# Softmax of an encoder step: minima of negated scores, maxima and low halves by turns, and a head's scaling moved to GpSimd

## What is computed

```
def sink_softmax(s, sink):
    m = jnp.maximum(jnp.max(s, axis=-1, keepdims=True), sink)
    e = jnp.exp(s - m)
    return e / (jnp.sum(e, axis=-1, keepdims=True) + jnp.exp(sink - m))
...
    s = jnp.einsum('bqkgd,bqskd->bkgqs', qg, kg).astype(jnp.float32) * SCALE
    s = jnp.where(valid[:, :, None, None, :], s, NEG)
    p = jax.nn.softmax(s, axis=-1)
```

## Time and profile before

| | |
|---|---|
| Median of three runs | 1899.58 us (1897.05 to 1901.8) |
| Profiled execution, its own time | 1900.48 us |
| Its span | 1898.7 us |
| PE busy | 1832.2 us (96% of the span) |
| DVE busy | 1112.3 us (59%) |
| ACT busy | 607.3 us (32%) |
| POOL busy | 372.4 us (20%) |

### The profile page before, as it was taken

How to read it: one execution, slowest core, us unless ns; L and a number is a source line. 1 busy time by engine, 2 the same in 40 slices (tenths; PEclk the granted TensorE clock), 3 DMA queues, 4 the chain that set the end, 5 groups by cost and what they waited for, 6 DMA issues and landing times.

```text
span 1898.7 us, 30572 instructions
## 1 busy us (share of the span) xinstructions
PE 1832.2 (96%) x11609; PEld 1780.1 (94%) x11609; DVE 1112.3 (59%) x1868; ACT 607.3 (32%) x1006; POOL 372.4 (20%) x299
## 2 busy tenths in 40 slices
PE   5999999999999998989899999999999999999997
PEld 4899999989999997777899999999999999999997
DVE  6257878978788686889663444553244452245443
ACT  4232122268511226777724211111011111011132
POOL 2112212256533324222320001110001110011100
PEclk8999999999999999999999999999999999999998
DMA  4111111110111114211213111111111111111112
GB/s 145 34 34 46 39 34 50 49 35 23 34 50 50 37 45 107 51 34 46 62 51 137 44 36 53 44 44 50 50 34 44 44 44 56 44 34 46 45 42 93
DMA packets 167458, 96.73 MB, mean 51 GB/s; under 512 B 7676, under 2 KB 163596, under 8 KB 167372
## 3 DMA queue, kind: packets, MB, share of 16 engines
q1 hardware_dynamic: 166396, 93.57, 17.0%
q0 software_dynamic: 976, 2.00, 0.4%
HBM read 89.55 MB, written 5.99 MB: 50 GB/s over the span
## 4 chain that ended last, share of the span: by engine, by line
PE 89%; DVE 5%; ACT 2%; issue 2%; DMA 1%; POOL 1%; SPq 0%; DVEq 0%; ACTq 0%
PE ps L954 75%; PE ps L1063 3%; PE ps L966 3%; PE ps L1086 3%; PE ps L1201 2%; PE ps L1161 2%; DVE probs L2078 1%; DVE key_mask L1893 1%; DVE top L1893 1%; DMA x_rows<-in_x_prompt 0%; PE ps L1027 0%; DVE h_rows L1814 0%; ACT probs L1549 0%; PE ps L1028 0%; DMA w_raw_in_lo<-in_w_in 0%
## 5 line engine op out<-in xcount | busy, mean ns | idle before, releaser
L954 PE MATMUL ps<-h_hi,w_hi 128*128 128x352 f32 (+1 forms) x1944 | 424.4, 326 | 3.9 <-POOL w_lo L770 3.9
L954 PE MATMUL ps<-h_hi,w_lo 128*128 128x352 f32 (+1 forms) x1944 | 420.3, 324 | 0.0
L954 PE MATMUL ps<-h_lo,w_hi 128*128 128x352 f32 (+1 forms) x1944 | 420.0, 324 | 0.0
L954 PEld LDWEIGHTS ps<-h_hi,w_hi 128*128 128x128 f32 (+1 forms) x1944 | 330.4, 189 | 6.8 <-issue 5.1
L954 PEld LDWEIGHTS ps<-h_hi,w_lo 128*128 128x128 f32 (+1 forms) x1944 | 334.1, 188 | 0.5
L954 PEld LDWEIGHTS ps<-h_lo,w_hi 128*128 128x128 f32 (+1 forms) x1944 | 330.8, 188 | 0.5
L1334 ACT ACTIVATE w_hi<-w_raw 128x1024 fp32r<-128x1024 f32 (+1 forms) x128 | 124.2, 971 | 245.7 <-PE ps L954 245.5
L923 POOL TENSOR_TENSOR t<-t,t 128x1056 f32<-128x1056 f32 x22 | 54.3, 2469 | 631.4 <-ACT t L1695 631.4
L1893 DVE MAX8 top<-key_mask 128x8 f32<-128x768 f32 (+5 forms) x192 | 170.6, 890 | 11.8 <-PE ps L954 1.2
L770 POOL TENSOR_TENSOR w_lo<-w_raw,w_hi 128x1024 fp32r<-128x1024 f32 (+1 forms) x53 | 100.5, 1896 | 354.5 <-ACT w_hi L1334 354.5
L1893 DVE MATCH_REPLACE8 key_mask<-top,key_mask 128x768 f32<-128x768 f32 (+5 forms) x192 | 167.8, 877 | 0.9 <-issue 0.9
(11 more groups left out here) (266 smaller groups left out, 2968.0 us busy)
## 6 DMA issues: line engine op xcount, KB each, us to landing
w_raw_in_lo<-in_w_in SPq DMA_DIRECT2D x56, 256.0 KB, 2.8
w_raw<-in_w_in SPq DMA_DIRECT2D x54, 256.0 KB, 3.0
w_raw<-in_w_gate SPq DMA_DIRECT2D x44, 256.0 KB, 3.0
w_raw<-in_w_up SPq DMA_DIRECT2D x44, 256.0 KB, 3.0
w_raw<-in_w_down SPq DMA_DIRECT2D x32, 256.0 KB, 2.9
w_raw_in_lo<-in_w_in SPq DMA_DIRECT2D x44, 128.0 KB, 2.2
x_rows<-in_x_prompt SPq DMA_DIRECT2D x8, 512.0 KB, 8.3
w_raw<-in_w_out SPq DMA_DIRECT2D x16, 256.0 KB, 3.1
```

The costliest lines, as they stand in the source:

```text
L954: last = nc.tensor.matmul(PS[0:rows, NB * k + b, 0:e - a], w[:, k, t, 0:rows], x[:, t, a:e], start=m == 0 and w is WHI and x is hi, stop=m ...
```

## The change

1. `mask_max` scales by −SCALE and keeps the minimum of the negated scores, which is the negated maximum, straight in the place that `exp` reads as its bias; `exp` scales by −1. In the window attention the reduction starts from the negated sink, in the sparse one from 3.4e38. The masks are added as before. The negations L2083, the combining operation L2106, the copies of the sample's sinks and the semaphore `negated` go; `exp` waits for its own head's maximum.
2. In sparse steps the two maxima stand by turns with the low halves: maximum 0, low half 0 (and in odd steps the running sum), maximum 1, low half 1. For pairs that are one ahead both reciprocals move in front of low half 2.
3. For the sixteen pairs that are one ahead, head 0 is scaled by POOL, behind the split of chunk 2 where there is one.

```
@@ pairs
-                            mask = None if window else MASK_S[:, :]
-                            sinks, negative = SINK_S[:, :], NEG_SINK[:, NH:NH + NKV]
+                            mask = MASK0[:, 0:n] if window else MASK_S[:, :]
+                            negative = NEG_SINK[:, NH:NH + NKV]
@@ POOL
-                    nc.gpsimd.tensor_copy(columns, pair["sinks"].unsqueeze(2)).then_inc(sink_in, 1)
+                    nc.gpsimd.tensor_copy(columns, pair["negative"].unsqueeze(2)).then_inc(sink_in, 1)
...
             def normalise(pair):
-                pool.wait_ge(inverse, 2 * pair["x"] + 2)
+                pool.wait_ge(inverse, 2 * pair["x"] + (2 if pair["window"] else 1))
                 p = probs_of(pair, 0)
                 inv = stat[:, pair["ub"], 5, 0:1].broadcast_to([P, pair["n"]])
                 nc.gpsimd.tensor_tensor(p, p, inv, ALU.mult).then_inc(probs[0], 1)
...
             for y, pair in enumerate(SPARSE):
-                for c in range(len(pair["chunks"])):
-                    sparse_split(y, c)
+                after = SPARSE[y + 1] if y + 1 < len(SPARSE) else None
+                for c in range(max(len(pair["chunks"]), 3)):
+                    if c < len(pair["chunks"]):
+                        sparse_split(y, c)
+                    if c == 2 and after and after["ahead"] == 1:
+                        normalise(after)
@@ ACT, exp
-                act.wait_ge(negated, 2 * x + (2 if pair["window"] else h + 1))
+                act.wait_ge(masked, 2 * x + h + 1)
...
-                nc.scalar.activation(p, p, ACT.Exp, bias=stat[:, ub, 1, h:h + 1],
+                nc.scalar.activation(p, p, ACT.Exp, scale=-1.0, bias=stat[:, ub, 1, h:h + 1],
@@ DVE, mask_max
-                top, neg = stat[:, ub, 0, h:h + 1], stat[:, ub, 1, h:h + 1]
-                out = probs_of(pair, h)
-                if pair["mask"] is None:
-                    V_.tensor_scalar(out, scores_of(pair, h), SCALE, None, ALU.mult, ALU.max,
-                                     accum_out=top).then_inc(masked, 1)
-                else:
-                    V_.tensor_tensor_reduce(out=out, in0=scores_of(pair, h), in1=pair["mask"], scale=SCALE,
-                                            scalar=-3.4e38, op0=ALU.add, op1=ALU.max,
-                                            accum_out=top).then_inc(masked, 1)
-                if not window:
-                    dve.wait_ge(masked, 2 * x + h + 1)
-                    V_.tensor_scalar(neg, top, -1.0, None, ALU.mult).then_inc(negated, 1)
+                V_.tensor_tensor_reduce(out=probs_of(pair, h), in0=scores_of(pair, h), in1=pair["mask"], scale=-SCALE,
+                                        scalar=pair["negative"][:, h:h + 1] if window else 3.4e38,
+                                        op0=ALU.add, op1=ALU.min,
+                                        accum_out=stat[:, ub, 1, h:h + 1]).then_inc(masked, 1)
@@ DVE, invert
-                if h == 0:
+                if h == 0 and pair["ahead"] == 2:
@@ DVE, window_step
-                    dve.wait_ge(masked, 2 * x + 2)
-                    V_.scalar_tensor_tensor(stat[:, ub, 1, :], stat[:, ub, 0, :], -1.0, ahead["negative"],
-                                            ALU.mult, ALU.min).then_inc(negated, 2)
@@ DVE, attend
-                        if ahead:
-                            mask_max(ahead, 0)
-                            mask_max(ahead, 1)
                         for c in range(max(count, 4)):
+                            if c < 2 and ahead:
+                                mask_max(ahead, c)
+                            if c == 2 and after and not early:
+                                invert(after, 0)
+                                invert(after, 1)
                             if c < count:
                                 pt_low(pair, c)
                             if c == 0 and y > 0 and ps[y - 1]["last"]:
                                 output(ps[y - 1])
-                            if c <= 1 and after and not early:
-                                invert(after, c)
```

More of the change, by code:

```diff
@@ L346, in build @@
         SINK = keep("sinks", NH)
-        SINK_S = keep("sinks_sample", NKV)
         TOP8 = keep("top8", 24)
@@ L386, in build @@
         q_hi = sem("q_hi")
-        s_done, masked, negated, exp_done = sem("s_done"), sem("masked"), sem("negated"), sem("exp_done")
+        s_done, masked, exp_done = sem("s_done"), sem("masked"), sem("exp_done")
         sink_in, inverse = sem("sink_in"), sem("inverse")
@@ L495, in pairs @@
                             head = g * NJ + 2 * half
-                            sinks, negative = SINK[:, head:head + 2], NEG_SINK[:, head:head + 2]
+                            negative = NEG_SINK[:, head:head + 2]
                         size = 1 if sample else 2
@@ L500, in pairs @@
                         out.append(dict(x=x, i=i, g=g, half=half, sample=sample, window=window, n=n,
-                                        first=first_block, chunks=chunks, q=q, mask=mask, sinks=sinks, negative=negative, ub=x % 3,
+                                        first=first_block, chunks=chunks, q=q, mask=mask, negative=negative, ub=x % 3,
                                         o=o, last=sample or half == 1))
@@ L1825, in _ @@
             for j in range(NJ):
-                V_.tensor_copy(SINK_S[DEC * j:DEC * (j + 1), :], SINK[DEC * j:DEC * (j + 1), j:NH:NJ])
                 V_.tensor_scalar(NEG_SINK[DEC * j:DEC * (j + 1), NH:NH + NKV],
@@ L2101, in window_step @@
                 if ahead:
-                    x, ub = ahead["x"], ahead["ub"]
                     mask_max(ahead, 0)
                     mask_max(ahead, 1)
-                    dve.wait_ge(masked, 2 * x + 2)
-                    V_.scalar_tensor_tensor(stat[:, ub, 1, :], stat[:, ub, 0, :], -1.0, ahead["negative"],
-                                            ALU.mult, ALU.min).then_inc(negated, 2)
                 if pair:
```

## The result

| | before | changed |
|---|---|---|
| Median | 1899.37 us (15 runs, 1897.05 to 1904.21) | 1904.84 us (15 runs, 1902.46 to 1910.97) |
| Ratio | | 1.0031, 95% interval 1.0022 to 1.0041 |
| Profiled execution, its own time | 1900.48 us | 1904.03 us |
| Span | 1898.7 us | 1902.2 us |

The account below looks back on a forecast made before the run. PE bounds the window stage; some 22 us of PE idle in the sparse stage is all the change can win. Terms 0 + 5.3 − 0.5 − 5.5 + 1.2 = +0.5 us gave 1900.1 us, range 1891 to 1908.

Parts of the forecast that it names:

- Tiles 0 and 1: Eight one-chunk steps: the second maximum behind the running sum delays PE's scores at four places; net +5.3 us.
- the 2.0 that I took: Tiles 0 and 1: part of the 7.3 us delay given back, as 2.9 us of old waits are already over.
- Tiles 3 and 4: Two-chunk steps: the later maximum is not late and low halves come one maximum earlier; −0.5 us.
- Tiles 5 to 7: Eleven steps: DVE loses negations and head 0's scaling, and the running sum comes earlier; net −5.5 us.
- the four steps with a split: Steps 17, 18, 19 and 23: GpSimd's scaling behind its split of chunk 2 ends late for PE's transposes; together +0.8 us.
- Step 17: In tiles 5 to 7: split plus scaling end at 824.6, against transposes starting at 822.72; +1.9 us.
- the −6.3 of the seven other steps: Tiles 5 to 7, steps without a split: each gains the lesser of PE's idle time and DVE's lost work.
- Tile 2: Two chunks, 384 keys: GpSimd's 0.83 us scaling replaces DVE's 0.42 on the chain in three of four pairs; +1.2 us.
- A: Rival: all of DVE's relief counts, all 11.96 us of idle time in tiles 5 to 7 goes; 1891.5 us, chance 0.21.
- B: Rival: sum before second maximum costs the full +7.3 in tiles 0 and 1, GpSimd scales slowly; 1907.7 us, chance 0.16.
- C: Rival: DVE and GpSimd stop each other, GpSimd's scaling holding DVE up for its whole length; 1913.6 us, chance 0.05.
- D: Rival: nothing measurable because no part reaches PE; 1899.6 us, chance 0.58 together with the forecast.

Follow-up runs that it names:

- kernels 2: The changed kernel with, for pairs two ahead, the order maximum 0, low half 0, maximum 1, running sum; 1900.0 us.
- Experiment 3: The changed kernel with head 0 scaled by DVE again for all sparse pairs; 1903.8 us.
- 10: The changed kernel profiled once more, nothing altered; 1904.3 us (one run).
- kernels 5: The changed kernel with GpSimd's scaling ahead of its split of chunk 2 instead of behind it; 1903.3 us.
- 9: The kernel before with turns in the steps that prepare pairs two ahead (tiles 0 to 4) and nothing else; 1909.1 us.
- Experiment 4: The kernel before with minima of negated scores alone: no negations, no turns, head 0 scaled by DVE, reciprocals where they were; 1896.0 us.
- kernel 1: The changed kernel with both maxima ahead of the low half again for pairs two ahead (tiles 0 to 4); 1895.7 us.
- kernel 7: As kernel 6, but GpSimd scales head 0 of pairs 17 to 28, ahead of its split of chunk 2; 1891.1 us.
- kernel 6: Minima everywhere, turns and later reciprocals only in steps preparing pairs 17 to 28, both maxima first elsewhere, head 0 scaled by DVE; 1893.0 us.

## Why the prediction was right in its range and short in its sum

**Tiles 0 and 1: the wait was right, the clock was left out.** Forecast +5.3, measured +7.7. The four places where PE's scores wait for the second maximum are in the trace of the changed kernel where they were forecast:

```profile
736.70 0.33 PE L1164 MATMUL ps<-k_hi,q_hi 64*128 64x128 f32 x2 [1.01 <-DVE softmax_stats L2074]
...
745.20 0.39 PE L1164 MATMUL ps<-k_hi,q_hi 64*128 64x256 f32 x2 [2.46 <-DVE softmax_stats L2074]
...
754.68 0.39 PE L1164 MATMUL ps<-k_hi,q_hi 64*128 64x256 f32 x2 [2.57 <-DVE softmax_stats L2074]
...
765.38 0.50 PE L1164 MATMUL ps<-k_hi,q_hi 64*128 64x512 f32 x2 [2.01 <-DVE softmax_stats L2074]
```

They are 1.0, 2.5, 2.6 and 2.0 us, in sum 8.1. At the third PE had waited before, too, for 0.9 us:

```profile
748.91 0.39 PE L1161 MATMUL ps<-k_hi,q_hi 64*128 64x256 f32 x2 [0.93 <-DVE softmax_stats L2078]
```

So 1.0, 2.5, 1.6 and 2.0 are new, in sum 7.1; forecast were 1.1, 2.3, 1.7 and 2.2, in sum 7.3. At the place of the earlier trace rows the chain reads as it was written: ACT's copy, DVE's sum, the maximum, and 0.06 us behind its end PE's scores at 745.20.

```profile
743.50 0.59 ACT L1337 ACTIVATE attn_sum<-ps 64x512 f32<-64x512 f32 x1
...
744.12 0.68 DVE L2124 TENSOR_TENSOR attn_sum<-ps,attn_sum 64x512 f32<-64x512 f32 x1 [3.43 <-ACT attn_sum L1337]
...
744.73 0.41 DVE L2074 CUSTOM_DVE_ANT_0 probs<-ps,mask_causal 128x256 f32<-128x256 f32 x1
```

Of this 1.2 is given back, not the 2.0 that I took: the two other old waits for maxima (2.0 us together) are still there with 1.8, and what went is a wait of 1.0 put down to issue. 7.1 − 1.2 makes, with rounding, the 6.0 us of new idle time. So the net term was 0.7 short by what is given back, and the missing 1.7 is the lower clock, which stands nowhere in my sum. Here are two pieces of tiles 0 and 1 of the changed kernel, and two of tile 2:

```profile
740.00:745.00 5.00, 2.75 (x25) 2.54 (x23) 1.45 (x5) 3.02 (x8) 2.55 (x2) 1.00 0.52 133
745.00:750.00 5.00, 4.80 (x30) 4.67 (x31) 3.18 (x13) 3.92 (x11) 2.52 (x2) 0.68 0.12 28
940.00:944.00 4.00, 2.70 (x18) 2.25 (x17) 2.31 (x7) 3.02 (x8) 2.12 (x2) 1.00 0.11 32
944.00:948.00 4.00, 3.64 (x16) 3.67 (x17) 0.69 (x1) 2.28 (x6) 1.28 (x1) 0.60 0.00 0
```

In 740 to 745 PE was busy for 2.75 of 5 us, at 1.00. In the next five it was busy for 4.80, with a granted clock of 0.68, so for most of them at the lower of its two levels, 1.2 GHz instead of 2.4. The same again in tile 2: 2.70 of 4 us busy, then 0.60. In both places the holes come first and the work behind them is slow. That makes a hole dearer than its length. How much dearer differs: against the 32.7 us of the kernels whose clock stays at 1.00, PE is busy for 1.7 to 1.9 us longer in kernels 2, 3, 10 and the changed one, and for 4.5 in kernels 5 and 9, which idle 10.2 and 10.5 us in tiles 0 and 1 where the changed one idles 10.2. That the holes bring the lower clock fits every profile here; no run changed one and held the other.

**Tiles 3 and 4.** Forecast −0.5, measured −1.1. Experiment 4 shows 0.9 of it with minima alone; I had counted the negations in tiles 5 to 7 only. The turns themselves gave 0.3 there (43.7 in experiments 1 and 4, 43.5 changed).

**Tiles 5 to 7: the size was right, its parts were not.** Forecast −5.5, measured −5.3. By parts: minima −3.4 (experiment 4), turns and late reciprocals −3.0 (experiment 3 against 4), GpSimd's scaling as placed +1.1 (the change against experiment 3). These parts are what each gave when added in this order; GpSimd's scaling without turns was not run. I had taken the scaling's relief of DVE for the main gain. What I had of it at the four steps with a split was right: the scaling's durations are those worked out from the slope, 1.46, 1.67, 1.89 and 0.83,

```profile
L829 POOL TENSOR_TENSOR probs<-probs,softmax_stats 128x1024 f32<-128x1024 f32 x4 | 7.6, 1894 | 1.8 <-DVE softmax_stats L2084 1.8
L829 POOL TENSOR_TENSOR probs<-probs,softmax_stats 128x896 f32<-128x896 f32 x4 | 6.7, 1684 | 1.0 <-DVE softmax_stats L2084 1.0
L829 POOL TENSOR_TENSOR probs<-probs,softmax_stats 128x768 f32<-128x768 f32 x4 | 5.9, 1464 | 1.0 <-DVE softmax_stats L2084 1.0
...
L829 POOL TENSOR_TENSOR probs<-probs,softmax_stats 128x384 f32<-128x384 f32 x4 | 3.3, 828 | 1.4 <-DVE softmax_stats L2084 1.4
```

and the splits push it past the start of the transposes. Step 17, at which I expected +1.9 (without taking off its idle 0.5, as I did at the other three): the split, the scaling, two search operations of DVE beside it, and then PE's transposes.

```profile
828.08 1.30 POOL L778 TENSOR_TENSOR w_lo<-w_raw_in_lo,w_hi 128x512 fp32r<-128x512 f32 x1 [3.89 <-ACT w_hi L1337]
...
829.33 1.47 POOL L829 TENSOR_TENSOR probs<-probs,softmax_stats 128x768 f32<-128x768 f32 x1
829.53 0.56 DVE L1895 MAX8 top<-key_mask 128x8 f32<-128x384 f32 x1
...
830.27 0.54 DVE L1895 MATCH_REPLACE8 key_mask<-top,key_mask 128x384 f32<-128x384 f32 x1
...
830.86 0.66 PE L969 MATMUL ps<-ident,probs 128*128 128x128 f32 x4 [1.61 <-POOL probs L829]
```

PE's transposes had to wait 1.6 us there, 1.6 and 1.3 in the next two steps, and 0.4 in step 23, against 1.9, 1.7, 0.85 and 0.1 of overshoot in the forecast. What failed inside the term is the −6.3 of the seven other steps: it took DVE's whole loss, up to 1.3 us a step, as PE's gain. That −5.5 came so near to −5.3 is luck: the negations and the turns gave 6.4, and the scaling, which I had taken for the main gain, cost 1.1. Experiment 3 has the scaling on DVE and eleven steps of 97.5 us, and with GpSimd's scaling well placed they take 95.6 (kernels 5 and 7): 8 us of DVE's work, taken away, gave PE 1.9.

**Tile 2: the cause was wrong.** Forecast +1.2 for GpSimd's slower scaling, measured +2.6: 1.0 more idle time and 1.6 more busy time, of which 1.4 is the clock (29.57 us busy in kernel 1, at 1.00, against 30.93). Experiment 3 keeps the waits with DVE's scaling and has 34.3, where experiment 4 has 32.6. Of these 1.7, 0.6 is there in kernel 6 without turns in tile 2, so it must come from the changed stretch ahead, and 1.1 belongs to the turns with the later reciprocals. GpSimd's scaling, with 34.0 in kernel 1 against 34.3, is 0.3 the better one: my term had the wrong sign.

**The sum.** +0.5 was forecast, +3.8 is what the four stretches show, and 3.1 of the 3.3 between them is clock (1.7 in tiles 0 and 1, 1.4 in tile 2). The other errors (+0.7 in tiles 0 and 1, −0.6 in 3 and 4, +0.2 in 5 to 7) nearly cancel. The medians are 5.5 apart, since the profiled execution of before was 1.1 above its median and that of the changed kernel 0.8 below.

**The rivals.** A (all of DVE's relief is PE's gain) is out: PE still idles 7.5 us in tiles 5 to 7, and even in kernel 7, where no split is in the way, 4.2. B was right in its place: the sum in front of the second maximum. Its terms for GpSimd at a slow pace were not: 1024 took 1.89 us, not 2.44 (and its sum leaves out the −0.5 of tiles 3 and 4). C is out: in the fence above a search maximum and a replacement of DVE, 0.56 and 0.54, ran beside GpSimd's scaling at their usual length (552 and 543 ns on average), and a low half of 512 that ran beside one (853.48, within the scaling of 853.07 to 854.75) took 0.69 us, the average being 0.69 too. The Trainium skill (SBUF — State Buffer, "SBUF: two separate sides") names DVE operations in a 2-port mode or with two inputs from SBUF as those that meet GpSimd, and these rows agree that a search or a low half, which reads one operand from PSUM, isn't among them. What did stretch is DVE's own scaling, from SBUF to SBUF: at 256 elements it took, in the changed kernel, 1.11 us at 748.87, during a weight split of GpSimd's, and 0.35 at 745.25, when GpSimd was idle. D is out too: the parts reach PE, and cancel.

## What to carry to other kernels

Before an instruction is moved behind another on its engine, ask what that other one waits for: one that waits for the very engine that waits for the moved one closes a circle, and its price is the whole chain, here 1.0 to 2.6 us at each of four places and, with the clock, more than the whole change won elsewhere (8.1 against 6.4). An order that wins in one regime of a loop (several chunks a step, one pair ahead) can lose in another, so it's to be chosen for each of them by its own stretch of the profile, and offloaded work goes ahead of whatever in the new engine's queue isn't urgent. And where PE starts to idle, look at its busy time for the same work, not only at its waits: a lower granted clock behind the holes added three tenths of their price here (1.7 on 6.0 us), and in two kernels three quarters.
